# The first layer's attention modulation: sums of products on VectorE, or columns of matmuls on TensorE

## The chip, the cores and the metric

The kernel runs on one core of one Trainium2 chip. The metric is the device time of one execution in microseconds (us), as the median of several runs. TensorE is called PE here, VectorE DVE, ScalarE ACT, GpSimd POOL; SP is the sync engine, whose queue issues nearly all DMAs.

## The reference, cut to what matters

Two transformer layers, then a third of another kind. All is float32, with 256 tokens and width D = 1024. Each of the first two layers begins with

```
c_act = silu(c)
mod = c_act @ ada_w[l] + ada_b[l]                 # (1024) x (1024, 6144)
sh_a, sc_a, g_a, sh_f, sc_f, g_f = split(mod, 6)
h = rms_norm(x, attn_norm_g[l]) * (1 + sc_a) + sh_a
mix = hybrid_mixer(h, ...)                        # projections, two kinds of attention
```

Only the first 2048 columns of the first layer's `ada_w` (shift and scale of the attention norm) are touched by this change in how they are multiplied. The other 4096 columns of that layer follow during the first mixer.

## The kernel before

x is kept transposed: channels on the 128 partitions, eight tiles of 256 tokens (`xT`, `hT`). All weights come from one DRAM array in slots of 128 x 2048 floats (1 MB) into a ring of 14 slots, in the order of use; `Loads.load` issues a slot's DMA from SP, first waiting until the place's last owner has been used, `Loads.ready` makes an engine wait for its landing, and `used` counts slots that are done with.

`stage_setup` (L350 to L400) loads c as a row spread over all partitions, the vector of small parameters `vec`, the constants `tab` (identity, ones), x, and eight "ada" slots. Here a slot holds 256 output channels: an output channel on each partition, its 1024 weights along the row, two such halves. ACT takes Silu of the row. DVE multiplies each half with the row and sums along it (L326, `dve_modulation`), which gives one column of `mod`; 16 products for eight slots, the first six slots ahead of the reciprocal of the norm, two behind it. Beside that, ACT squares x tile by tile, PE sums the squares over channels with a matrix of ones (`pe_sum`, L463), and ACT takes the root. PE then runs 32 fillers (`keep_warm`, L316: identity times identity into an unused bank, two instructions each, as for every float32 product). At the end DVE adds the bias (L341) and makes the amp, g (1 + scale) (L346). SP queues the first two slots of the mixer and the first four of twelve "late" ada slots behind the eight.

`stage_mixer` for layer 0 starts behind a barrier of all engines. DVE scales x by amp and norm (L499), ACT adds the shift (L505), and PE runs through `items`: two output tiles a slot from slots 0 to 3, latent sums after the fifth item, queries and keys from slots 4 and 5, values, and two tiles a slot from slots 6 to 9. ACT copies each result out of its bank. DVE, meanwhile, has angles (waiting for the positions `posi`), a forget gate, a norm of the latents, the rotation, and between them the twelve late slots with `modulation(...)`. SP's order there is: positions, row of c again, mixer slots 2 to 9, late slots 4 to 7 (each waits until DVE is done with the slot four before), and behind the forget rows the late slots 8 to 11 and the mixer's last four. Attention and the output product follow, then the dense layer, the second mixer, two mixtures of experts and the third layer.

Of the kernel before, what the change touches and what calls it, by code (L numbers as in the profile page):

```python
# [8 lines left out]
ALU = mybir.AluOpType  # L9
ACT = mybir.ActivationFunctionType  # L10
# [4 lines left out]
P = 128  # L15
D = 1024
DT = D // P
T = 256
TT = T // P
SLOT = 2048  # L20
# [10 lines left out]
def vector_columns():  # L31

    cols = []
    for l in range(2):
        cols += [(f"ada_b{l}", 48), (f"attn_g{l}", 8), (f"ffn_g{l}", 8), (f"q_g{l}", 2), (f"kv_g{l}", 1),
                 (f"mla_g{l}", 4), (f"fox_g{l}", 4), (f"forget_b{l}", 1)]
    cols += [("final_g", 8), ("norm1", 8), ("norm2", 8), ("mu_prev", 14), ("mu_next", 14), ("decay0", 8),
             ("gate0", 8), ("k_k", 4), ("k_a", 4), ("r_k", 4), ("gn_w", 4), ("gn_b", 4), ("qn_g", 1),
             ("kn_g", 1), ("b_merge", 16)]
    at, out = 0, {}  # L40
    for name, n in cols:
        out[name] = slice(at, at + n)
        at += n
    return out, at
# [267 lines left out]
def keep_warm(k, bank, n):  # L312

    ident = k.t("ident")
    for _ in range(n):
        k.nc.tensor.matmul(bank[:, 0:P], ident, ident, start=True, stop=True)  # L316


def dve_modulation(k, dve, loads, slots, l, c_row, product, link, first=0):


    for j in slots:
        w = loads.ready(dve, j)
# [12 lines left out]
ADA_FIRST, ADA_LATE = 8, 12  # L336


def dve_bias(k, l, span, link):
    bias = k.vec[:, VEC[f"ada_b{l}"].start + span.start:VEC[f"ada_b{l}"].start + span.stop]  # L340
    link(k.nc.vector.tensor_tensor(k.mod[:, l, span], k.mod[:, l, span], bias, ALU.add))  # L341
# [5 lines left out]
                                          ALU.add, ALU.mult))  # L347


def stage_setup(k, loads, nxt, side):  # L350

    nc = k.nc
    small = k.counter("small_arrived")
    act_step = k.counter("act_step")
    x_arrived = k.counter("x_arrived")
    c_row, product = (k.hT[:, i:i + 4, :].rearrange("p t n -> p (t n)") for i in (0, 4))
    norm = StreamNorm(k, k.bank[0])
    with nc.Block() as block:
        @block.sync
        def _(sp):  # L360
            sp.dma_start(c_row, k.dram["c_row"].partition_broadcast(P)).then_inc(*small.up(16))
            sp.dma_start(k.vec[:, :], k.dram["vec"][:, :]).then_inc(*small.up(16))
            for j in range(4):
                loads.load(sp, j)
            sp.dma_start(k.tab[:, :], k.dram["tab"][:, :]).then_inc(*x_arrived.up(16))
            sp.dma_start(k.xT[:, :, :], k.dram["xT"][:, :, :]).then_inc(*x_arrived.up(16))
            for j in range(4, loads.n):
                loads.load(sp, j)
            sp.dma_start(k.router["router1"], k.dram["router1"][:, :, :]).then_inc(*k.counter("router_arrived").up(16))
            nxt.load(sp, 0)  # L370
            nxt.load(sp, 1)
            side.head(sp)

        @block.scalar
        def _(act):
            act.wait_ge(*small.at(32))
            nc.scalar.activation(c_row, c_row, ACT.Silu).then_inc(*act_step.up())
            act.wait_ge(*x_arrived.at(32))
            for t in range(DT):
                norm.act_square(act, t, k.xT[:, t, :])  # L380
            act.wait_ge(*norm.square_used.at(DT))
            norm.act_root(act)

        @block.tensor
        def _(pe):
            pe.wait_ge(*x_arrived.at(32))
            for t in range(DT):
                norm.pe_sum(pe, t, norm.bank, t == 0, t == DT - 1)
            keep_warm(k, k.bank[7], 32)

        @block.vector
        def _(dve):
            link = linker(dve, k.counter("dve_step"))
            dve.wait_ge(*act_step.at(1))
            dve_modulation(k, dve, loads, range(6), 0, c_row, product, link)
            norm.dve_inverse(dve, link)
            dve_modulation(k, dve, loads, range(6, ADA_FIRST), 0, c_row, product, link)
            dve_bias(k, 0, slice(0, 2 * ADA_FIRST), link)
            dve_amp(k, 0, 0, link)
    k.close()  # L400

# [146 lines left out]
def stage_mixer(k, l, loads, nxt, norm, nxt_norm, side=None):  # L548
    nc = k.nc
    S = k.counter  # L550
    dve_step, act_step = S("dve_step"), S("act_step")
    tile_done, tile_out = S("tile_done"), S("tile_out")
    with ExitStack() as ctx:
# [32 lines left out]
        forget_step, forget_moved = S("forget_step"), S("forget_moved")  # L586
        with nc.Block() as block:
            @block.sync
            def _(sp):
                sp.dma_start(k.posi[:, :], k.dram["pos1"].partition_broadcast(P)).then_inc(*S("small_arrived").up(16))  # L590
                if side is not None:
                    sp.dma_start(ada_c, k.dram["c_row"].partition_broadcast(P)).then_inc(*S("ada_arrived").up(16))
                    for j in range(2, 10):
                        loads.load(sp, j)
                    for j in range(side.slots, 2 * side.slots):
                        side.load(sp, j)
                sp.wait_ge(*S("pool_step").at(2))
                sp.wait_ge(*forget_step.at(4))
                sp.dma_start(qf[64:65, :, :], scratch[0:8, 6, :]).then_inc(*forget_moved.up(16))
                sp.dma_start(kf[96:97, :, :], scratch[0:8, 7, :]).then_inc(*forget_moved.up(16))  # L600
                if side is not None:
                    for j in range(2 * side.slots, side.n):
                        side.load(sp, j)
                    for j in range(10, loads.n):
                        sp.wait_ge(*side.done(side.n - side.slots + j - 10))
                        loads.load(sp, j)
                loads.rest(sp)
                sp.wait_ge(*forget_moved.at(32))
# [103 lines left out]
            def _(dve):  # L712
                v = nc.vector
                link = linker(dve, dve_step)

                def modulation(*js):
                    if side is not None:
                        if js[0] == 0:
                            dve.wait_ge(*act_step.at(1))
                        dve_modulation(k, dve, side, js, l, ada_c, ada_product, link, ADA_FIRST)  # L720
# [1 line left out]
                if l:  # L722
                    norm.dve_inverse(dve, link)
                norm.dve_scale(k.hT, k.amp[:, l, 0, :], norm.scaled)
                dve.wait_ge(*S("small_arrived").at(16))
                dve_angles(k, link, cos, sin, scratch[:, 0, :], scratch[:, 1, :], k.t("freq1"))
                v.tensor_copy(scratch[:, 2, :], cos[:, :]).then_inc(*S("angle_ready").up())
                modulation(0, 1)
                dve.wait_ge(*tile_out.at(4))
                link(v.tensor_scalar(z, misc[0:8, :], k.v(f"forget_b{l}")[0:8, :], None, ALU.add))  # L730
                link(v.tensor_scalar(lo, z, 0.0, None, ALU.min))
# [7 lines left out]
                for t in range(2):  # L739
# [1 line left out]
                                           ALU.mult).then_inc(*lat_ready.up())  # L741
                v.scalar_tensor_tensor(ckv[:, 0, :], ckv[:, 0, :], k.v(f"kv_g{l}", 0), k.rstd[:, 1, :], ALU.mult,
                                       ALU.mult).then_inc(*lat_ready.up())
                modulation(2, 3)
                dve.wait_ge(*forget_step.at(2))
                link(v.tensor_tensor(lo, lo, e, ALU.subtract))
                v.tensor_tensor_scan(F, k.t("ones")[0:8, 0:1].broadcast_to([8, T]), lo, 0.0, ALU.mult,
                                     ALU.add).then_inc(*forget_step.up())
                dve.wait_ge(*forget_step.at(3))
                v.tensor_scalar(negF, F, -1.0, None, ALU.mult).then_inc(*forget_step.up())  # L750
                modulation(4, 5)
                modulation(6, 7, 8)
                dve.wait_ge(*S("trig_ready").at(1))
                for i in range(5):
                    if i < 4:
# [718 lines left out]
TILE = 32  # L1474
QUADS = P // TILE
# [1881 lines left out]
def program(nc, dram, out):  # L3357
    with ExitStack() as ctx:
# [27 lines left out]
        def after(name):  # L3386
            if name == "mix1":
                return wide
            at = names.index(name) + 1
            return loads[names[at]] if at < len(names) else Loads(k.weights, 0)  # L3390

        stage_setup(k, loads["ada"], after("ada"), late_ada)
        norms = {name: (TokenNorm if name == "moe2" else StreamNorm)(k, k.bank[b]) for name, b in (
            ("mix0", 0), ("dense", 5), ("mix1", 4), ("moe1", 5), ("hybrid", 0), ("moe2", 0))}
        stage_mixer(k, 0, loads["mix0"], after("mix0"), norms["mix0"], norms["dense"], late_ada)
# [230 lines left out]
```

## Time and profile before

| | us |
|---|---|
| median of 3 runs | 2361.96 |
| lowest, highest | 2361.61, 2366.49 |
| the profiled execution | 2362.96 |
| its span, first to last instruction | 2360.7 |
| PE busy | 2185.4 (93% of the span) |
| DVE busy | 665.5 (28%) |
| ACT busy | 317.1 (13%) |

Times in the profile are counted from the first instruction. The rows below name the engine, the line, the operation and the tiles (out<-in); in brackets stand the idle time ahead of a group and what ended it. PE's float32 products appear as two instructions each.

### The profile page before, as it was taken

The page shows a single profiled execution, that of the slowest core. Times are in us where ns is not written, and L with a number is a line of the kernel's source. Part 1 is how long each engine was busy: PE and PEld are TensorE (multiplying, and loading weights), DVE is VectorE, ACT ScalarE, POOL GpSimd, SP SyncE. Part 2 cuts the span into 40 slices and gives each one's busy share as a digit, 9 for nine tenths or more (in the row PEclk, how much of TensorE's full clock was granted, in tenths as well). Part 3 has the DMA queues.
Part 4 walks back from the last instruction along what each step waited for, and adds up shares of the span by engine and source line. Part 5 has one row for each costly group of instructions (what it writes and reads, how often), then busy time and mean ns, then how long its engine had stood idle before and what let it go on. Part 6 is the DMA issues. An engine that isn't in the chain of part 4 may idle for free. (4 is left out here: it accounts for less than half of the span.)

```text
span 2360.7 us, 46236 instructions
## 1 busy us (share of the span) xinstructions
PE 2185.4 (93%) x21328; PEld 1336.0 (57%) x21328; DVE 665.5 (28%) x1237; ACT 317.1 (13%) x711; POOL 30.9 (1%) x30
## 2 busy tenths in 40 slices
PE   6999999999999999999999999999999997767776
PEld 5788888887734344443535353678889862212221
DVE  6863222344501101011011012237554331111110
ACT  2431000144200000000000000143232110000000
POOL 1000000010000000000000000100000000000000
PEclk9999999999999999999999999999999998777777
DMA  9668555701699999999999999634400679999998
GB/s 399 255 252 336 210 228 214 304 37 55 252 398 414 406 400 416 403 419 400 420 400 419 394 420 418 252 134 143 151 25 4 264 323 421 421 421 422 421 422 361
DMA packets 111595, 734.83 MB, mean 311 GB/s; under 512 B 12832, under 2 KB 16192, under 8 KB 36768
## 3 DMA queue, kind: packets, MB, share of 16 engines
q1 hardware_dynamic: 109456, 724.82, 75.8%
q8 instruction: 171, 2.80, 0.5%
q0 software_dynamic: 1152, 4.19, 0.4%
q10 hardware_dynamic: 784, 2.75, 0.3%
q14 instruction: 32, 0.26, 0.0%
HBM read 721.20 MB, written 10.09 MB: 310 GB/s over the span
## 5 line engine op out<-in xcount | busy, mean ns | idle before, releaser
L1550 PE MATMUL bank<-ring,moe_xg 128*32 128x512 f32 (+1 forms) x6144 | 580.8, 540 | 0.7 <-DVE moe_xg L1706 0.7
L1550 PEld LDWEIGHTS bank<-ring,moe_xg 128*32 128x32 f32 x6144 | 199.1, 110 | 377.1 <-issue 375.1
L1561 PE MATMUL bank<-ring,moe_turned 128*32 128x256 f32 x5376 | 291.5, 379 | 0.0
L1561 PEld LDWEIGHTS bank<-ring,moe_turned 128*32 128x32 f32 x5376 | 174.7, 110 | 117.1 <-issue 3.1
L1104 PE MATMUL bank<-h_chan,ring 128*128 128x256 f32 x896 | 195.6, 379 | 1.4 <-ACT h_chan L505 1.4
L1104 PEld LDWEIGHTS bank<-h_chan,ring 128*128 128x128 f32 x896 | 170.2, 190 | 24.7 <-issue 1.6
L2062 PE MATMUL bank<-ring,late 128*32 128x512 f32 x696 | 118.2, 779 | 56.1 <-DMA ring<-stream 56.0
L1745 DVE TENSOR_TENSOR moe_hidden<-moe_silu,bank 128x512 f32<-128x512 f32 (+1 forms) x48 | 26.9, 616 | 482.2 <-PE bank L1550 482.2
L2513 PE MATMUL bank<-h_chan,ring 128*128 128x256 f32 x624 | 137.2, 380 | 0.0
L2513 PEld LDWEIGHTS bank<-h_chan,ring 128*128 128x128 f32 x624 | 118.0, 190 | 18.9 <-issue 3.3
L2062 PEld LDWEIGHTS bank<-ring,late 128*32 128x32 f32 x696 | 17.5, 121 | 150.2 <-DMA ring<-stream 129.7
L1088 PE MATMUL bank<-dense_hidden,ring 128*128 128x256 f32 x448 | 98.8, 379 | 0.0
L1699 DVE COPY moe_y<-bank 32x256 f32<-32x256 f32 x48 | 20.0, 416 | 257.1 <-PE bank L1561 256.6
L1088 PEld LDWEIGHTS bank<-dense_hidden,ring 128*128 128x128 f32 x448 | 85.1, 190 | 11.6
L632 PE MATMUL bank<-h_chan,ring 128*128 128x256 f32 x384 | 84.0, 379 | 1.0 <-ACT h_chan L505 1.0
L2085 PE MATMUL bank<-ring,moe_turned 128*32 128x512 f32 x392 | 59.2, 708 | 26.5 <-DMA ring<-stream 25.5
L1607 ACT ACTIVATE moe_silu<-bank 128x512 f32<-128x512 f32 (+1 forms) x48 | 22.7, 545 | 434.5 <-PE bank L1550 434.5
L632 PEld LDWEIGHTS bank<-h_chan,ring 128*128 128x128 f32 x384 | 72.8, 190 | 11.8 <-issue 2.1
L2128 DVE TENSOR_TENSOR moe_hidden<-late,bank 128x512 f32<-128x512 f32 x8 | 5.5, 687 | 239.4 <-PE bank L2062 239.4
L326 DVE CUSTOM_DVE_ANT_0 ada_product<-ada_slots,ada_c 128x1024 f32<-128x1024 f32 x56 | 68.5, 1223 | 1.5
L1121 DVE TENSOR_TENSOR dense_hidden<-dense_silu,bank 128x512 f32<-128x512 f32 x14 | 9.6, 688 | 201.3 <-PE bank L1104 201.3
L1690 ACT ACTIVATE moe_y<-bank 32x256 f32<-32x256 f32 x48 | 18.1, 376 | 354.2 <-PE bank L1561 353.7
(461 smaller groups left out, 2064.4 us busy)
## 6 DMA issues: line engine op xcount, KB each, us to landing
ring<-stream SPq DMA_DIRECT2D x257, 1024.0 KB, 22.5
ring<-wide SPq DMA_DIRECT2D x240, 1024.0 KB, 15.9
ring<-wide SPq DMA_DIRECT2D x128, 768.0 KB, 15.8
late<-stream SPq DMA_DIRECT2D x47, 1024.0 KB, 27.0
ada_slots<-stream SPq DMA_DIRECT2D x28, 1024.0 KB, 7.1
h_chan<-stream SPq DMA_DIRECT2D x9, 1024.0 KB, 26.7
rows<-zeros SPq DMA_DIRECT2D x8, 512.0 KB
moe_x_rows<-rows SPq DMA_DIRECT2D x28, 96.0 KB, 9.0
```

The costliest lines, as they stand in the source:

```text
L326: mul = k.nc.vector.tensor_tensor_reduce(product, w[:, i * D:(i + 1) * D], c_row, 1.0, 0.0, ALU.mult, ALU.add, accum_out=k.mod[:, l, at:at ...
L632: mm = nc.tensor.matmul(b[:, 0:T], w[:, t, i * P:(i + 1) * P], k.hT[:, t, :], start=(t == 0), stop=(t == DT - 1))
L1088: mm = nc.tensor.matmul(k.bank[t // 2][:, (t % 2) * T:(t % 2) * T + T], w[:, f, t * P:(t + 1) * P], hidden[:, c % 2, f, :], start=(c == 0 ...
L1104: mm = nc.tensor.matmul(b[:, f * T:(f + 1) * T], w[:, t, f * P:(f + 1) * P], k.hT[:, t, :], start=(t == 0), stop=(t == DT - 1))
L1550: mm = self.k.nc.tensor.matmul(banks[r][i * TILE:(i + 1) * TILE, 0:width], self.m.xg[:, r, t * TILE:(t + 1) * TILE], w[:, i, :], start=(t ...
L1561: mm = self.k.nc.tensor.matmul(self.sum_bank[r][q * TILE:(q + 1) * TILE, :], self.m.turned[:, r, n * TILE:(n + 1) * TILE], w[:, f2, q * T: ...
L1607: k.nc.scalar.activation(m.silu[:, r, 0:self.span[c]], self.gate_bank[r][:, 0:self.span[c]], ACT.Silu)\
L1699: last = self.k.nc.vector.tensor_copy(self.m.y[r * TILE:(r + 1) * TILE, q * T:(q + 1) * T], self.sum_bank[r][q * TILE:(q + 1) * TILE, :])
L1745: v.tensor_tensor(m.hidden[:, r, 0:self.span[c]], m.silu[:, r, 0:self.span[c]], self.up_bank[r][:, 0:self.span[c]], ALU.mult).then_inc(*se ...
L2062: mm = k.nc.tensor.matmul((self.gate_bank if j < self.per_proj else self.up_bank)[own, :], m.xg[:, t, own], w[:, i, e, :], start=(t == 0), ...
L2085: mm = k.nc.tensor.matmul(k.bank[half][own, :], m.turned[:, f, own], w[:, i, e, :], start=(f == 0), stop=(f == 3))
L2513: mm = nc.tensor.matmul(b[:, 0:T], lhsT, rhs, start=(t == 0), stop=(t == DT - 1))
```

## The change

The eight ada slots of the first layer now hold rows by input channel: slot j has input channels 128j to 128j+127 on the partitions and all 2048 output channels along the row. c comes as eight columns inside `vec`, not as a row; ACT takes Silu of them, each spread over 32 columns (`c_blocks`, 128 x 8 x 32). PE multiplies for each slot four times, 128x32 by 512 columns, into four groups of 32 partitions of one bank, summed over the eight slots. One filler stands ahead of the first slot and eight ahead of each of the others. DVE copies the bank to SBUF, PE turns the rows to columns with four products against four columns of the identity, and DVE adds the bias. The reciprocal of the norm stands ahead of all that on DVE.

SP's order: `vec`, `tab`, x, the eight slots, positions, router, two mixer slots. The late slots leave the setup: in the mixer's block the row of c comes first, then late slots 0 and 1, then mixer slots 2 to 7 and late slots 2 to 7 in turn, then mixer slots 8 and 9. DVE takes late slot 2 ahead of the forget gate; 3 and 4, 5 and 6, 7 and 8 follow at the places after.

```diff
-def stage_setup(k, loads, nxt, side):
+def stage_setup(k, loads, nxt):
...
         def _(sp):
-            sp.dma_start(c_row, k.dram["c_row"].partition_broadcast(P)).then_inc(*small.up(16))
             sp.dma_start(k.vec[:, :], k.dram["vec"][:, :]).then_inc(*small.up(16))
-            for j in range(4):
-                loads.load(sp, j)
             sp.dma_start(k.tab[:, :], k.dram["tab"][:, :]).then_inc(*x_arrived.up(16))
             sp.dma_start(k.xT[:, :, :], k.dram["xT"][:, :, :]).then_inc(*x_arrived.up(16))
-            for j in range(4, loads.n):
+            for j in range(loads.n):
                 loads.load(sp, j)
+            sp.dma_start(k.posi[:, :], k.dram["pos1"].partition_broadcast(P)).then_inc(*posi_arrived.up(16))
...
             nxt.load(sp, 0)
             nxt.load(sp, 1)
-            side.head(sp)
...
-            act.wait_ge(*small.at(32))
-            nc.scalar.activation(c_row, c_row, ACT.Silu).then_inc(*act_step.up())
+            act.wait_ge(*small.at(16))
+            nc.scalar.activation(c_blocks, spread_last(k.v("c"), TILE), ACT.Silu).then_inc(*act_step.up())
...
                 norm.pe_sum(pe, t, norm.bank, t == 0, t == DT - 1)
-            keep_warm(k, k.bank[7], 32)
+            pe.wait_ge(*act_step.at(1))
+            for j in range(loads.n):
+                keep_warm(k, k.bank[7], 8 if j else 1)
+                w = loads.ready(pe, j)
+                for q in range(QUADS):
+                    mm = nc.tensor.matmul(row_bank[q * TILE:(q + 1) * TILE, :], c_blocks[:, j, :],
+                                          w[:, q * 512:(q + 1) * 512], start=(j == 0), stop=(j == DT - 1))
+                mm.then_inc(*((k.used, 1)))
+            pe.wait_ge(*rows_out.at(1))
+            for i in range(QUADS):
+                mm = nc.tensor.matmul(column_bank[:, i * QUADS:(i + 1) * QUADS], rows[:, i * P:(i + 1) * P],
+                                      k.t("ident")[:, 0:P:TILE], start=True, stop=True)
+            mm.then_inc(*turned.up())
...
-            dve.wait_ge(*act_step.at(1))
-            dve_modulation(k, dve, loads, range(6), 0, c_row, product, link)
             norm.dve_inverse(dve, link)
-            dve_modulation(k, dve, loads, range(6, ADA_FIRST), 0, c_row, product, link)
-            dve_bias(k, 0, slice(0, 2 * ADA_FIRST), link)
+            dve.wait_ge(*posi_arrived.at(16))
+            dve.wait_ge(*loads.done(loads.n - 1))
+            v.tensor_copy(rows, row_bank[:, :]).then_inc(*rows_out.up())
+            dve.wait_ge(*turned.at(1))
...
+            link(v.tensor_tensor(own, columns, bias, ALU.add))
             dve_amp(k, 0, 0, link)
...
-                if side is not None:
+                if side is None:
+                    sp.dma_start(k.posi[:, :], k.dram["pos1"].partition_broadcast(P))\
+                        .then_inc(*S("small_arrived").up(16))
+                else:
                     sp.dma_start(ada_c, k.dram["c_row"].partition_broadcast(P)).then_inc(*S("ada_arrived").up(16))
-                    for j in range(2, 10):
+                    side.load(sp, 0)
+                    side.load(sp, 1)
+                    for j in range(2, 8):
                         loads.load(sp, j)
-                    for j in range(side.slots, 2 * side.slots):
                         side.load(sp, j)
+                    for j in range(8, 10):
+                        loads.load(sp, j)
...
                 modulation(0, 1)
+                modulation(2)
...
-                modulation(2, 3)
+                modulation(3)
+                modulation(4)
...
-                modulation(4, 5)
-                modulation(6, 7, 8)
+                modulation(5, 6)
+                modulation(7, 8)
```

## Rows read from the trace of the kernel before

**Rows 1.** The page's head.
```profile
span 2360.7 us, 46236 instructions
```

**Rows 2.** Timeline, 0 to 75 us: start, duration, engine, line, operation, out<-in, count.
```profile
0.73 0.39 SPq L361 DMA_DIRECT2D h_chan<-c_row  x1
...
3.64 1.28 SPq L365 DMA_DIRECT2D tab_sb<-tab  x1
...
8.52 1.22 DVE L326 CUSTOM_DVE_ANT_0 h_chan<-ring,h_chan 128x1024 f32<-128x1024 f32 x1 [8.52 <-DMA ring<-stream]
...
19.47 1.03 ACT L458 ACTIVATE rstd<-x_chan 128x256 f32<-128x256 f32 x3 [12.63 <-DMA x_chan<-xT]
...
20.03 6.32 PE L463 MATMUL bank<-rstd,tab_sb 128*128 128x256 f32 x16 [20.03 <-ACT rstd L458]
...
22.06 1.23 DVE L326 CUSTOM_DVE_ANT_0 h_chan<-ring,h_chan 128x1024 f32<-128x1024 f32 x1 [3.44 <-DMA ring<-stream]
...
26.19 7.31 PE L316 MATMUL bank<-tab_sb 128*128 128x128 f32 x64
...
34.20 0.17 DVE L346 SCALAR_TENSOR_TENSOR amp<-mod,vec_sb 128x8 f32<-128x8 f32 x1
...
36.09 17.51 PE L632 MATMUL bank<-h_chan,ring 128*128 128x256 f32 x80
...
45.70 0.29 DVE L843 CAST score<-posi 128x256 f32<-128x256 int32 x1 [7.53 <-DMA posi<-pos]
```

**Rows 3.** Windows: engines' busy time, PEclk (granted), DMA share, GB/s.
```profile
0.00:6.00 6.00, 0.00 (x0) 0.00 (x0) 0.00 (x0) 1.50 (x2) 0.19 (x4) 1.00 0.62 202
6.00:20.00 14.00, 0.00 (x0) 0.00 (x1) 9.86 (x16) 1.37 (x3) 0.00 (x0) 1.00 1.01 426
20.00:34.00 14.00, 13.46 (x80) 12.12 (x80) 11.63 (x18) 4.34 (x9) 0.00 (x0) 1.00 1.01 418
```

**Rows 4.** Timeline at the end of the first mixer block.
```profile
92.06 13.98 PE L635 MATMUL bank<-ring,h_chan 128*128 128x256 f32 x64
...
103.29 0.17 DVE L346 SCALAR_TENSOR_TENSOR amp<-mod,vec_sb 128x8 f32<-128x8 f32 x1
106.07 0.38 ACT L697 ACTIVATE vf<-bank 128x256 f32<-128x256 f32 x1 [3.07 <-PE bank L635]
```

**Rows 5.** Line L463: ns min/median/max, first and last start.
```profile
L463 PE MATMUL bank<-rstd,tab_sb x16: 379/634/767, 20.0 to 26.0; 128*128 128x256 f32 x16
```

**Rows 6.** PE's timeline in the last stage, 1910 to 2000 us.
```profile
1918.12 7.07 PE L2062 MATMUL bank<-ring,late 128*32 128x512 f32 x64
1925.01 1.90 PE L2062 MATMUL bank<-late 128*32 128x512 f32 x16
...
1931.02 1.04 PE L2062 MATMUL bank<-ring,late 128*32 128x512 f32 x8
1931.99 0.44 PE L2031 MATMUL bank<-tab_sb,moe_gated 128*128 128x128 f32 x2
...
1934.49 1.95 PE L2046 MATMUL bank<-moe_pick,late 128*128 128x128 f32 x16
1936.37 2.78 PE L2085 MATMUL bank<-ring,moe_turned 128*32 128x512 f32 x24
```

**Rows 7.** Timeline of the last stage, 1990 to 2010 us: column products copied out.
```profile
1992.61 1.06 PE L2085 MATMUL bank<-ring,moe_turned 128*32 128x512 f32 x8 [0.80 <-DMA ring<-stream]
...
1993.74 0.69 DVE L2139 COPY moe_y<-bank 128x512 f32<-128x512 f32 x1 [9.21 <-PE bank L2085]
```

**Rows 8.** Timeline ahead of the last stage: small products, and DVE reading a bank.
```profile
1904.13 1.05 PE L518 MATMUL bank<-tab_sb,rstd 128*128 128x1 f32 x8
...
1907.54 0.22 DVE L1360 SCALAR_TENSOR_TENSOR moe_gl<-bank,moe_inverse,mod 128x4 f32<-128x4 f32 x1 [0.40 <-PE bank L1326]
```

**Rows 9.** DMA issues, 0 to 80 us: KB each, us to landing.
```profile
h_chan<-c_row SPq DMA_DIRECT2D x1, 512.0 KB, 3.7
```

More of the change, by code:

```diff
@@ L37, in vector_columns @@
     cols += [("final_g", 8), ("norm1", 8), ("norm2", 8), ("mu_prev", 14), ("mu_next", 14), ("decay0", 8),
-             ("gate0", 8), ("k_k", 4), ("k_a", 4), ("r_k", 4), ("gn_w", 4), ("gn_b", 4), ("qn_g", 1),
+             ("gate0", 8), ("c", 8), ("k_k", 4), ("k_a", 4), ("r_k", 4), ("gn_w", 4), ("gn_b", 4), ("qn_g", 1),
              ("kn_g", 1), ("b_merge", 16)]
@@ L347, in dve_amp @@
                                           ALU.add, ALU.mult))
-def stage_setup(k, loads, nxt, side):
[L352 to L356, printed above, removed]
+def stage_setup(k, loads, nxt):
+    nc, S = k.nc, k.counter
+    small, x_arrived, posi_arrived = S("small_arrived"), S("x_arrived"), S("forget_moved")
+    act_step, rows_done, rows_out, turned = S("act_step"), S("tile_done"), S("tile_out"), S("rot_done")
+    c_blocks = k.hT[:, 0, :].rearrange("p (t n) -> p t n", t=DT)
+    rows = k.hT[:, 4:6, :].rearrange("p t n -> p (t n)")
+    row_bank, column_bank = k.bank[6], k.bank[5]
     norm = StreamNorm(k, k.bank[0])
@@ L360, in _ @@
         def _(sp):
-            sp.dma_start(c_row, k.dram["c_row"].partition_broadcast(P)).then_inc(*small.up(16))
             sp.dma_start(k.vec[:, :], k.dram["vec"][:, :]).then_inc(*small.up(16))
-            for j in range(4):
-                loads.load(sp, j)
             sp.dma_start(k.tab[:, :], k.dram["tab"][:, :]).then_inc(*x_arrived.up(16))
             sp.dma_start(k.xT[:, :, :], k.dram["xT"][:, :, :]).then_inc(*x_arrived.up(16))
-            for j in range(4, loads.n):
+            for j in range(loads.n):
                 loads.load(sp, j)
-            sp.dma_start(k.router["router1"], k.dram["router1"][:, :, :]).then_inc(*k.counter("router_arrived").up(16))
+            sp.dma_start(k.posi[:, :], k.dram["pos1"].partition_broadcast(P)).then_inc(*posi_arrived.up(16))
+            sp.dma_start(k.router["router1"], k.dram["router1"][:, :, :]).then_inc(*S("router_arrived").up(16))
             nxt.load(sp, 0)
             nxt.load(sp, 1)
-            side.head(sp)
         @block.scalar
         def _(act):
-            act.wait_ge(*small.at(32))
-            nc.scalar.activation(c_row, c_row, ACT.Silu).then_inc(*act_step.up())
+            act.wait_ge(*small.at(16))
+            nc.scalar.activation(c_blocks, spread_last(k.v("c"), TILE), ACT.Silu).then_inc(*act_step.up())
             act.wait_ge(*x_arrived.at(32))
@@ L388, in _ @@
                 norm.pe_sum(pe, t, norm.bank, t == 0, t == DT - 1)
-            keep_warm(k, k.bank[7], 32)
+            pe.wait_ge(*act_step.at(1))
[11 more added lines that the diff above has]
+            mm.then_inc(*turned.up())
         @block.vector
         def _(dve):
-            link = linker(dve, k.counter("dve_step"))
-            dve.wait_ge(*act_step.at(1))
-            dve_modulation(k, dve, loads, range(6), 0, c_row, product, link)
+            v = nc.vector
+            link = linker(dve, S("dve_step"))
             norm.dve_inverse(dve, link)
-            dve_modulation(k, dve, loads, range(6, ADA_FIRST), 0, c_row, product, link)
-            dve_bias(k, 0, slice(0, 2 * ADA_FIRST), link)
+            dve.wait_ge(*posi_arrived.at(16))
+            dve.wait_ge(*loads.done(loads.n - 1))
+            v.tensor_copy(rows, row_bank[:, :]).then_inc(*rows_out.up())
+            dve.wait_ge(*turned.at(1))
+            own = k.mod[:, 0, 0:2 * ADA_FIRST].rearrange("p (g i) -> p i g", g=QUADS)
+            bias = k.v("ada_b0")[:, 0:2 * ADA_FIRST].rearrange("p (g i) -> p i g", g=QUADS)
+            columns = column_bank[:, 0:2 * ADA_FIRST].rearrange("p (i g) -> p i g", g=QUADS)
+            link(v.tensor_tensor(own, columns, bias, ALU.add))
             dve_amp(k, 0, 0, link)
@@ L589, in _ @@
             def _(sp):
-                sp.dma_start(k.posi[:, :], k.dram["pos1"].partition_broadcast(P)).then_inc(*S("small_arrived").up(16))
-                if side is not None:
+                if side is None:
+                    sp.dma_start(k.posi[:, :], k.dram["pos1"].partition_broadcast(P))\
+                        .then_inc(*S("small_arrived").up(16))
+                else:
                     sp.dma_start(ada_c, k.dram["c_row"].partition_broadcast(P)).then_inc(*S("ada_arrived").up(16))
-                    for j in range(2, 10):
+                    side.load(sp, 0)
+                    side.load(sp, 1)
+                    for j in range(2, 8):
                         loads.load(sp, j)
-                    for j in range(side.slots, 2 * side.slots):
                         side.load(sp, j)
+                    for j in range(8, 10):
+                        loads.load(sp, j)
                 sp.wait_ge(*S("pool_step").at(2))
@@ L724, in _ @@
                 norm.dve_scale(k.hT, k.amp[:, l, 0, :], norm.scaled)
-                dve.wait_ge(*S("small_arrived").at(16))
+                if side is None:
+                    dve.wait_ge(*S("small_arrived").at(16))
                 dve_angles(k, link, cos, sin, scratch[:, 0, :], scratch[:, 1, :], k.t("freq1"))
@@ L3390, in after @@
             return loads[names[at]] if at < len(names) else Loads(k.weights, 0)
-        stage_setup(k, loads["ada"], after("ada"), late_ada)
+        stage_setup(k, loads["ada"], after("ada"))
         norms = {name: (TokenNorm if name == "moe2" else StreamNorm)(k, k.bank[b]) for name, b in (
@@ L3544 @@
                       ("gate0", "a_gate0_2"), ("k_k", "k_k_2"), ("k_a", "k_a_2"), ("r_k", "r_k_2"),
-                      ("gn_w", "gn_w_2"), ("gn_b", "gn_b_2"), ("b_merge", "b_merge_2")):
+                      ("gn_w", "gn_w_2"), ("c", "c"), ("gn_b", "gn_b_2"), ("b_merge", "b_merge_2")):
         put(name, x[key])
@@ L3555 @@
     for l in range(2):
-        add(x["ada_w"][l].T.reshape(24, 2, P, D).transpose(0, 2, 1, 3).reshape(24, P, SLOT))
+        rows = 0
+        if l == 0:
+            add(x["ada_w"][0][:, 0:SLOT].reshape(DT, P, SLOT))
+            rows = SLOT
+        add(x["ada_w"][l][:, rows:].T.reshape(-1, 2, P, D).transpose(0, 2, 1, 3).reshape(-1, P, SLOT))
     def mixer(l):
```

## Prediction

> **What bounds the kernel now.** I read the page's head first [rows 1], then the first 45 us in order of time [rows 2], what the DMA engines moved there [rows 3], and the first mixer block's end [rows 4]. The reader is to see that after 36 us TensorE (PE) is the engine that everything waits for: the mixer's first products start at 36.09, its last ones (64 instructions of L635) run from 92.06 to 106.04, and ScalarE's last copy of them at 106.07 ends the block, with VectorE (DVE) done at 103.46 [rows 2, 4]. In those 70 us PE waits for nobody for more than 0.5 us at a time, and no slot is late. So the change is worth what it does to one moment: the end of the setup's amp at 34.20 + 0.17 = 34.37, which starts the scaling, the shift and, 1.7 us later, PE [rows 2]. Before that moment DVE is the bound: it waits for the fifth slot until 22.06 and then multiplies without a gap. All that follows hangs on PE's start, so I take a shift of that moment one to one to the end.
>
> **The transfers.** In the first 6 us 202 GB/s x 6 = 1.21 MB move, then about 0.42 MB per us [rows 3], so a slot of 1.05 MB every 2.49 us. Up to the first slot 1.71 MB were asked for (row of c, vec, slot), which the rates give at 7.2; DVE began on it at 8.52. Up to the fifth slot it is 7.42 MB, at 20.8; DVE began at 22.06 [rows 2]. Both lag by 1.3 us, and I use that as the landing delay. In the new order vec, tab and xT are 1.64 MB, so xT is there at 6 + 0.43/0.42 + 1.3 = 8.4; as the first microseconds could be slower with a table in front of them, 8.5. It was 19.47. The last of eight slots: 10.03 MB, 6 + 8.82/0.42 + 1.3 = 28.3.
>
> **PE before the slots.** The eight sums of squares took from 19.47 to the first filler at 26.19, 6.72 us [rows 2]. They ran mostly at the lower clock: the granted clock reads 1.00, but the L463 instructions last 634 ns in the median and 379 at the least [rows 5], and ScalarE's squares behind them are 0.85 us apart; that is the 1.2 GHz level, and PE had stood idle 20 us before. The same idle lies ahead of them after the change (8.5 us), so 6.72 again: PE reaches the slots at 15.2, with two of them landed.
>
> **PE at the slots.** Per slot there are now eight fillers (16 instructions of 128x128 by 128 columns) and four products of 128x32 by 512 columns in four column groups (8 instructions). Before has no such mixture in the setup, but its last stage has both halves with the switch between them [rows 6]: from the last set of eight L2062 to the next full-width instruction 1931.99 - 1931.02 = 0.97 us, and from 16 full-width instructions of L2046 to the next column set 1936.37 - 1934.49 = 1.88. Together 2.85 us a slot. That is more than the 2.49 us of its transfer, so PE never catches up with the loads. The first slot has one filler: 0.22 + 0.1 + 0.97 = 1.3. The slots end at 15.2 + 1.3 + 7 x 2.85 = 36.45, and the last set of products starts 0.97 ahead of it, at 35.5.
>
> Sets that follow each other show what the switch is: eight of them start 1925.01 - 1918.12 = 6.89 us apart, 0.86 each [rows 6], so 0.11 of the 0.97 us is the switch. With the same on the way back, 16 switches are 1.8 us in all. The Trainium skill has a rule for this that speaks against the change: on the page TensorEngine Tiling (Array Packing), section Key Properties, it says that going to another tiling mode, unlike going to another tile, drains the engine. The trace agrees, with 0.11 us for one. Without such a drain the sum would be 1.8 us less, by that rule it is as above.
>
> **The tail.** Nearest is the last stage, where a set of column products is copied out of PSUM: set at 1992.61, copy of 128x512 at 1993.74 for 0.69 [rows 7]. So copy at 35.5 + 1.13 = 36.6 to 37.3. The four turning products (8 instructions with full weights and 4 columns) are nearest to L518, eight of 128x1 in 1.05 us [rows 8]; 0.05 to start, 0.1 until DVE sees them: 38.5. Bias from PSUM: 0.22, as L1360 [rows 8]; 0.03; amp 0.17 [rows 2]. The amp ends at 39.0 in place of 34.37: **4.6 us later**. Bounds of the unknown pieces: the sums at the upper clock throughout would take 3.5 us instead of 6.7 (their products at half the price; the squares at 0.42 each keep up), which leaves 1.4; a clock that rises 3 us later than it did costs about 1.5 more, 6.1; xT half a microsecond either way.
>
> **What is removed.** DVE loses 16 products of 1.22 us and their reads, the broadcast row of c (0.5 MB, 1.25 us of transfer) and its Silu of 1.06 us. These were the bound from 22.06 to 34.37; PE's 21 us in a row take that place, so they give back nothing more than is in the sum. The bias and amp stay.
>
> **The mixer's part** I cost at nothing, and this is the cover. SP no longer queues four late slots in the setup; the last thing there is the second mixer slot, 12.3 MB in, at 33.7. The engines then stand idle until the block starts. The row of c, issued at 39.5, lands as it did from an idle queue in 3.7 us [rows 9], 43.2; late slots 0 and 1 and mixer slot 2 follow, 50.7. PE starts at 39.0 + 1.7 = 40.7 and wants slot 2 after four items of 3.5 us, 54.7: 4.0 us to spare. From then on two slots come per 5.0 us and PE takes 6.9 us for one of the mixer's (17.51 us for five items [rows 2]), so the margin grows. Late slots 4 to 7 now wait in SP's queue for DVE's use of late slots 0 to 3, and mixer slots 5 to 9 wait behind them. The last gate is that of late slot 7: it opens with the products on late slot 3, which follow the latent norm, some 28 us after PE's start (the norm's last row is 26 us after it now); mixer slot 8 behind it is wanted 56 us after. DVE's own chain: the positions came only at 45.70, after 7.5 us of waiting, and are now there at once, so the angles and late slots 0 and 1 move ahead, and the 2.5 us of late slot 2 in front of the forget gate end before PE has delivered the latent sums. Late slot 8 is issued behind the forget rows as before and lands about 45 us after PE's start; the products on it end 47.5 us after, as now (83.6 - 36.1). So DVE keeps its 3 us ahead of PE at the end [rows 4]. If a late slot cost more than those, each microsecond would count.
>
> **Sum.** The profiled execution took 2362.96 us, 2.3 more than its span of 2360.7 [rows 1], and the median of the three runs is 1.0 below it. 2362.96 + 4.6 = 2367.6, less 1.0 is **2366.6**. A change under 0.2% (4.7 us) can't be told from none here; the forecast lies just within, so its two halves count for same and slower.
>
> **Rivals.**
> (a) *The loads set the pace*: the fillers fit into the gaps between landings. Then the last set starts at 28.3, the copy at 29.4 and the amp ends at 31.8, 2.6 us earlier: 2359.4, still same. For it speaks that the fillers stand ahead of each wait; against it 2.85 against 2.49 us and a start with two slots behind. It holds only if a slot costs PE under 1.7 us: (28.3 - 16.5)/7. Chance 0.10.
> (b) *The lower clock lasts*: PE's first burst now comes after 8.5 us, with ScalarE's pace between its sums. Should the clock rise 6 us later than the 5 us it took before, 6 us of the sums and first slots pass at half the rate, 3 us more, 7.6 in all: 2369.6, slower. It decides from 0.1 us beyond my sum on. Against it stands that the burst and the idle time ahead of it are of the same kind as before. With it a mixer slot 2 late by over 4 us, which would need the row of c to land 4 us later than in 3.7. Chance 0.15.
> (c) *Faster by over 0.2%*: the mixer would have to give back 9 us; DVE's end is 3 us clear of PE's, so there is nothing to win. Chance 0.03.
> (d) *Nothing arrives*: a later stage paced by its loads swallows the delay. The middle stages are full of PE work, and the last one starts when its slots come free; 2362. Chance 0.04.
>
> **Chances.** The forecast with 2363.5 to 2368 has 0.68, of which 0.40 lie within 0.2% and 0.28 above. Same: 0.40 + 0.10 + 0.04 = 0.54; slower: 0.28 + 0.15 = 0.43; faster 0.03. The range that leaves out 2 in 10: the lower end between rival (a) and the forecast, 2361.0, the upper with rival (b) nearly whole, 2369.5.
>
> **What would show it.** xT's squares start near 8.5; PE is busy without a wait from 15 to 36, with pairs of 1.88 and 0.97; slots have landed by 29 and wait for PE; the amp ends at 39; the mixer's first products start at 40.7 and last 70 us. Wrong if a slot costs PE less than 2.5 us, if the first sums are over before 13, if PE waits in the mixer for slot 2, or if the end of the block doesn't move with its start.

## Result, and the profile after

The changed kernel is slower: 2370.34 us in the median of eight runs against 2364.25 of eight runs of the kernel before, ratio 1.0029 (95% interval 1.0020 to 1.0038), so 6.9 us (4.7 to 9.0). In a second comparison it was 1.0034 (1.0022 to 1.0046). One of the first eight runs of the changed kernel, at 4490 us, lies so far off that the ratio leaves it out.

The timeline of the kernel after, 0 to 48 us, answers to [rows 2]; its last row is taken from the view of 41 to 62 us:

```profile
9.00 1.03 ACT L473 ACTIVATE rstd<-x_chan 128x256 f32<-128x256 f32 x3 [5.68 <-DMA x_chan<-xT]
9.56 6.15 PE L478 MATMUL bank<-rstd,tab_sb 128*128 128x256 f32 x16 [9.56 <-ACT rstd L473]
15.54 0.38 PE L316 MATMUL bank<-tab_sb 128*128 128x128 f32 x2
15.86 1.07 PE L392 MATMUL bank<-ring,h_chan 128*32 128x512 f32 x8
16.85 2.05 PE L316 MATMUL bank<-tab_sb 128*128 128x128 f32 x16
18.84 1.06 PE L392 MATMUL bank<-ring,h_chan 128*32 128x512 f32 x8
19.83 2.05 PE L316 MATMUL bank<-tab_sb 128*128 128x128 f32 x16
...
36.70 1.06 PE L392 MATMUL bank<-ring,h_chan 128*32 128x512 f32 x8
37.94 0.69 DVE L408 COPY h_chan<-bank 128x512 f32<-128x512 f32 x1 [19.75 <-PE bank L392]
38.69 1.05 PE L397 MATMUL bank<-tab_sb,h_chan 128*128 128x4 f32 x8 [0.92 <-DVE h_chan L408]
39.78 0.18 DVE L413 TENSOR_TENSOR mod<-bank,vec_sb 128x16 f32<-128x16 f32 x1 [1.15 <-PE bank L397]
40.00 0.17 DVE L346 SCALAR_TENSOR_TENSOR amp<-mod,vec_sb 128x8 f32<-128x8 f32 x1
40.70 1.43 PE L316 MATMUL bank<-tab_sb 128*128 128x128 f32 x10 [0.96 <-PEq L359]
...
41.91 19.14 PE L652 MATMUL bank<-h_chan,ring 128*128 128x256 f32 x80
```

x is there at 9.00 instead of 19.47, and PE begins with the slots at 15.54. Then fillers and products follow each other without a bracket, which means without idle time: from set to set 18.84 - 15.86 = 2.98 us, and 36.70 - 15.86 is seven times that. DVE, which had been the bound, sits for 19.75 us until the last set is done. The amp ends at 40.17 in place of 34.37, 5.8 us later.

The second thing to see is the last row. The mixer's first 80 instructions took 17.51 us before [rows 2] and take 19.14 now. The windows over PE at their start (columns: stretch, length, busy and count, PEclk, DMA share, GB/s) say why:

```profile
41.90:45.20 3.30, 3.30 (x10) 0.50 0.89 292
45.20:48.50 3.30, 3.30 (x17) 0.99 1.02 425
```

PE is busy in both, but the granted clock in the first is 0.50, the 1.2 GHz level, and 10 instructions pass instead of 17. Ahead of it PE had done little from 37.76 to 40.70: 0.92 us of waiting for the copy, eight instructions of 4 columns, 0.96 us of waiting for the new block. The ten fillers at the start of the block still passed in 1.43 us, and the clock fell at their end. The end of the first mixer block, answering to [rows 4]:

```profile
99.52 13.98 PE L655 MATMUL bank<-ring,h_chan 128*128 128x256 f32 x64
...
110.62 0.17 DVE L346 SCALAR_TENSOR_TENSOR amp<-mod,vec_sb 128x8 f32<-128x8 f32 x1
113.53 0.38 ACT L717 ACTIVATE vf<-bank 128x256 f32<-128x256 f32 x1 [3.07 <-PE bank L655]
114.22 1.97 PE L908 MATMUL bank<-km,qm 96*128 96x256 f32 x8 [0.73 <-PEq L602]
```

The attention's first products before:

```profile
106.76 3.69 PE L885 MATMUL bank<-km,qm 96*128 96x256 f32 x16 [0.73 <-PEq L587]
```

The last copy at 113.53 stood at 106.07: 7.46 us later, which is 5.8 + 1.65. DVE's last row there ends 2.7 us ahead of it; before it was 2.6. The attention's first product here, at 114.22, stood at 106.76; it is the mark by which the experiments are compared. Like every mark it is read from one profiled execution of each run, while the times are medians of several.

### The profile page after: what moved, and what is told of

It reads as the page before. It is cut to its first block and busy times, and to the rows that moved or that the text cites. A ratio compares the mean times of both kernels' runs of the same rounds, so it can differ in the third digit from the quotient of the medians.

```text
span 2370.4 us, 46440 instructions
## 1 busy us (share of the span) xinstructions
PE 2202.0 (93%) x21450; PEld 1343.0 (57%) x21450; DVE 649.9 (27%) x1206; ACT 317.0 (13%) x711; POOL 30.9 (1%) x30
```

## The experiments

Theory A: PE sets the pace of the new setup, because eight fillers, four products and two changes of shape take more than the 2.49 us in which a slot lands; in its second part, the pauses of PE around the turning (the four products that turn rows to columns) let the clock fall. Theory B: the loads moved out of the setup cost the time. Theory C was added when a result did not fit. The marks of each run, in us; "amp" is its end, "80" the mixer's first 80 instructions:

| run | amp | 80 | attention | ratio to before (95%) |
|---|---|---|---|---|
| before | 34.37 | 17.51 | 106.8 | |
| after | 40.17 | 19.14 | 114.2 | 1.0029 (1.0020 to 1.0038) |
| e11_after_again | 39.40 | 18.36 | 113.4 | 1.0034 (1.0022 to 1.0046) |
| e2_fillers0 | 31.88 | 18.32 | 105.9 | one run, 2362.93 us |
| e8_nofill_timed | 34.27 | 18.12 | 108.3 | 1.0008 (0.9999 to 1.0017) |
| e1_fillers4 | 32.61 | 18.17 | 106.6 | 1.0012 (1.0003 to 1.0021) |
| e10_fillers16 | 51.02 | 17.50 | 123.4 | 1.0092 (1.0077 to 1.0107) |
| e6_same_shape | 36.26 | 17.77 | 110.0 | one run, 2367.03 us |
| e3_warm_tail | 38.41 | 17.50 | 110.9 | 1.0026 (1.0017 to 1.0035) |
| e5_both | 33.44 | 17.50 | 105.9 | 1.0006 (0.9997 to 1.0015) |
| e12_two_same_shape | 33.97 | 17.50 | 106.5 | 1.0002 (0.9993 to 1.0010) |
| e4_order_alone | 34.34 | 17.50 | 106.7 | 1.0000 (0.9991 to 1.0009) |
| e9_delay | 42.16 | 17.50 | 114.5 | 1.0042 (1.0029 to 1.0056) |
| e7_vec_pad | 34.74 | 17.50 | 107.1 | 1.0004 (0.9995 to 1.0013) |

**Four fillers a slot.**

```diff
-                keep_warm(k, k.bank[7], 8 if j else 1)
+                keep_warm(k, k.bank[7], 4 if j else 1)
```

> The changed kernel with four fillers ahead of each slot's products instead of eight. Theory A (the setup is paced by TensorE: fillers, products and the changes of shape take 2.98 us a slot): a slot takes 2.98 - 0.89 = 2.09 us, less than the 2.49 us of its transfer, so the loads set the pace; the last set of products starts near 29 instead of 36.70 and the amp ends 3.3 us after that, near 32.5 instead of 40.00 + 0.17. Time 7.7 us below the changed kernel if TensorE's clock in the mixer behaves as it did there, ratio to the kernel before 0.9995 (0.9985 to 1.0005). Theory B (the loads taken out of the setup, and the transfer engines idle between the blocks, cost the time): the setup is shorter, but the mixer waits for slots and gives it back; ratio stays above 1.002.

The timeline of this run, last two sets and what follows:

```profile
27.07 1.06 PE L392 MATMUL bank<-ring,h_chan 128*32 128x512 f32 x8
28.06 1.16 PE L316 MATMUL bank<-tab_sb 128*128 128x128 f32 x8
29.15 1.06 PE L392 MATMUL bank<-ring,h_chan 128*32 128x512 f32 x8
...
33.14 2.31 PE L316 MATMUL bank<-tab_sb 128*128 128x128 f32 x10 [0.96 <-PEq L359]
35.25 18.17 PE L652 MATMUL bank<-h_chan,ring 128*128 128x256 f32 x80
```

A slot takes 2.08 us, the last set starts at 29.15 and the amp ends at 32.61: theory A's numbers, and theory B falls, for the mixer does not wait. One step of the expectation was not so: the loads don't set the pace here. From the first set at 14.56 to the last no row has a wait in front of it, so PE, which began behind its loads, still sets the pace and only just catches up. The gain of 1.8 us over the kernel before is gone by the attention, since the block's fillers and 80 instructions take 1.6 us more than before at the lower clock. But the time is 1.0012 of before, though attention starts 0.2 us earlier than there; theory A had 0.9995. That is theory C's ground, below.

**No fillers**, in one execution (e2) and in a timed run (e8).

```diff
-                keep_warm(k, k.bank[7], 8 if j else 1)
```

> The changed kernel without any filler between the slots. Theory A: loads set the pace as with four; the products of a set run at 1.2 GHz (1.73 us instead of 0.86), which still fits into 2.49 us; the last set starts near 29, the amp ends near 33.5; the mixer's first products run at the lower clock for some microseconds, costing 1.5 to 3 us there. Theory B: nothing is gained over the changed kernel at the end of the first mixer block (its first attention product at 114.2).

> No fillers between the slots, timed. Its one execution had attention at 105.9 and 2362.93 in all. Theory A: 0.9 us under the kernel before plus nothing, ratio 0.9996. Theory C: 2 us over it, ratio 1.0009.

The timeline of the first of them:

```profile
17.63 1.07 PE L391 MATMUL bank<-ring,h_chan 128*32 128x512 f32 x8 [1.00 <-DMA ring<-stream]
20.12 1.06 PE L391 MATMUL bank<-ring,h_chan 128*32 128x512 f32 x8 [1.42 <-DMA ring<-stream]
22.59 1.94 PE L391 MATMUL bank<-ring,h_chan 128*32 128x512 f32 x8 [1.41 <-DMA ring<-stream]
...
27.55 1.93 PE L391 MATMUL bank<-ring,h_chan 128*32 128x512 f32 x8 [0.54 <-DMA ring<-stream]
```

From the fourth on each set waits for its slot, 2.47 to 2.49 us apart, as worked out from the transfers. Three sets ran at the lower clock (1.93 in place of 1.06 us; the granted clock from 22.5 to 28 us is 0.50) and still fit. The amp ends at 31.88, and at 34.27 in the second execution, in which x and the slots landed 1.6 us later and the turning took 1.87 in place of 1.05 us. The time, 1.0008, can't be told from that of the kernel before; it is what theory C expected, but with the attention 1.6 us late in this execution it doesn't decide for it.

**Sixteen fillers a slot.**

```diff
-                keep_warm(k, k.bank[7], 8 if j else 1)
+                keep_warm(k, k.bank[7], 16 if j else 1)
```

> The changed kernel with sixteen fillers a slot instead of eight. Theory A: each slot takes 1.79 us more, 4.77, seven of them 12.5 us; the last set starts near 49.2 and the amp ends near 52.7; the time is 12.5 us above the changed kernel, ratio to the kernel before 1.008 (1.007 to 1.0095). Theory B: fillers lie in waits for slots, and the amp moves by clearly less than 12 us.

```profile
15.20 3.84 PE L316 MATMUL bank<-tab_sb 128*128 128x128 f32 x32
18.97 1.07 PE L392 MATMUL bank<-ring,h_chan 128*32 128x512 f32 x8
19.97 3.84 PE L316 MATMUL bank<-tab_sb 128*128 128x128 f32 x32
...
51.55 1.35 PE L316 MATMUL bank<-tab_sb 128*128 128x128 f32 x10 [0.96 <-PEq L359]
```

A slot takes 19.97 - 15.20 = 4.77 us, as expected. The amp ends at 51.02, not 52.7, because the first sums started at 8.00 here and at 9.56 in the execution it was worked out from. With 4, 8 and 16 fillers the slot is 2.08, 2.98 and 4.77: fillers are paid one to one while PE is behind the loads. The last row is for later: these are the mixer's ten fillers, at the upper clock (1.35 us as before).

**Fillers in the products' shape.**

```diff
-                keep_warm(k, k.bank[7], 8 if j else 1)
+                for _ in range(8 if j else 1):
+                    nc.tensor.matmul(k.bank[7][0:TILE, 0:P], c_blocks[:, 0, :], k.t("ident"), start=True, stop=True)
```

> The changed kernel with its eight fillers a slot in the shape of the products (weights 128x32 into one column group, 128 columns), so that TensorE doesn't change shape between fillers and products. Theory A with the change of shape as a cost of 0.1 us or more each way: a slot takes 16 x 0.107 + 0.86 = 2.6 us (2.55 to 2.75) instead of 2.98, the amp ends 2.6 us earlier in the same time after x has landed. If the change of shape costs nothing and the 2.98 are the instructions themselves: 2.9 us or more.

```profile
16.98 0.63 PE L393 MATMUL bank<-ring,h_chan 128*32 128x512 f32 x3
...
18.05 1.80 PE L390 MATMUL bank<-tab_sb,h_chan 128*32 128x128 f32 x15
19.58 0.63 PE L393 MATMUL bank<-ring,h_chan 128*32 128x512 f32 x3
```

The same 16 + 8 instructions take 2.60 us a slot in one shape and 2.98 in two. So 0.38 us of each slot, 2.7 us of seven, belong to the changes of shape and what goes with them: more than the 0.22 that I had read from the last stage.

**The clock around the turning.**

```diff
+            keep_warm(k, k.bank[7], 4)
             pe.wait_ge(*rows_out.at(1))
...
             mm.then_inc(*turned.up())
+            keep_warm(k, k.bank[7], 3)
```

> The changed kernel with four more fillers between the last slot's products and the turning, and three behind the turning. Theory A, its second part (the pauses of TensorE around the turning let the clock fall to 1.2 GHz in the mixer's first 3 us): the amp ends where it did, 40.2 (40.0 to 40.4); the mixer's first 80 instructions take 17.5 us as before instead of 19.14, and attention starts 1.6 us earlier than at 114.2; ratio to the kernel before 1.0022. If the lower clock there has another cause (the shape of the work ahead of it, or chance), the 80 instructions keep 19.1 us.

> The changed kernel once more, beside the others on one chip. Theory A: amp between 38.4 and 40.2 (with x landing between 8 and 9), the mixer's 80 instructions over 18 us again because of the pauses around the turning; ratio 1.0026 (1.002 to 1.0035). If the slow 80 instructions were chance: 17.5 us.

The last rows of the run with these fillers, then the windows over its first products:

```profile
37.84 0.91 PE L316 MATMUL bank<-tab_sb 128*128 128x128 f32 x6
38.24 0.17 DVE L346 SCALAR_TENSOR_TENSOR amp<-mod,vec_sb 128x8 f32<-128x8 f32 x1
39.05 1.35 PE L316 MATMUL bank<-tab_sb 128*128 128x128 f32 x10 [0.30 <-PEq L359]
40.24 17.50 PE L654 MATMUL bank<-h_chan,ring 128*128 128x256 f32 x80
```

```profile
40.20:43.50 3.30, 3.30 (x17) 1.00 0.93 298
```

The amp ended at 38.41, not near 40.2, because the sums began at 8.47 and took 5.3 us, against 9.56 and 6.0 in the execution the expectation was worked out from. So the amp says nothing on the fillers, and the stretch behind it is what counts. From the end of the amp to the attention it is 114.2 - 40.2 = 74.0 us in the changed kernel, 74.0 in its repetition and with four fillers, 74.0 and 74.1 in the runs without any, and 73.7 in the one with the other shape. It is 72.5 in every run with fillers around the turning (e3, e5, e12) and 72.4 in the kernels that turn nothing (before, e4, e9, e7). The second part of theory A holds: where the clock falls, it costs 1.3 to 1.7 us against 72.4. One run stands apart: with sixteen fillers a slot and the same pauses it is 72.4 too, so a pause makes the fall possible and not sure. In the time the 1.6 us can't be seen: 1.0026 against 1.0029 and 1.0034, with intervals of 0.0009 to 0.0012 either way.

**The order alone**, in the kernel before: late slots out of the setup, positions in, mixer and late slots in turn, and the new places on DVE.

```diff
+            sp.dma_start(k.posi[:, :], ...)
...
-            side.head(sp)
...
+                    side.load(sp, 0)
+                    side.load(sp, 1)
+                    for j in range(2, 8):
                         loads.load(sp, j)
                         side.load(sp, j)
```

> The kernel before with the new order alone: late slots out of the setup, positions in it, mixer and late slots in turn, and the new places of the late products on VectorE; the modulation of the first layer stays on VectorE. Theory A: costs nothing, the amp ends at 34.4 and attention starts at 106.7 within 0.4 us; ratio 1.000. Theory B: attention starts 2 us or more later, ratio 1.001 or more.

```profile
34.86 1.35 PE L316 MATMUL bank<-tab_sb 128*128 128x128 f32 x10 [2.35 <-PEq L358]
36.05 17.50 PE L638 MATMUL bank<-h_chan,ring 128*128 128x256 f32 x80
```

Attention at 106.7 and ratio 1.0000: the order costs nothing, as the prediction had it. The first row shows in passing that 2.35 us without any work, behind 64 dense instructions of fillers, left the clock up.

**What lies behind the mixer (theory C).** Two kernels on the base of the one before: eight unused columns in `vec`, and a delay.

```diff
-             ("gate0", 8), ("k_k", 4), ...
+             ("gate0", 8), ("spare", 8), ("k_k", 4), ...
```

> The kernel before with eight unused columns in the vector of parameters, where the change puts c, so that all that lies behind it in SBUF moves by 32 bytes a partition. Theory C with the layout as its cause: attention starts at 106.7 as before, but the end comes 2 to 4 us later, ratio 1.0013. Theory A, or C with another cause: ratio 1.000.

```diff
-            keep_warm(k, k.bank[7], 32)
+            keep_warm(k, k.bank[7], 64)
...
             dve_bias(k, 0, slice(0, 2 * ADA_FIRST), link)
+            for _ in range(6):
+                link(nc.vector.tensor_tensor(product, product, product, ALU.max))
```

> The kernel before with six more VectorE products of 1.23 us ahead of the amp (they change nothing that is read) and 32 more fillers on TensorE beside them, so that the amp ends 7.6 us later and TensorE is as busy ahead of the mixer as before. A delay there goes one to one to the end: 7.6 us later, ratio 1.0032 (1.0024 to 1.004). If the stages behind take part of a delay up, or add to it, it is under 5 or over 10 us.

The layout's 1.0004 (0.9995 to 1.0013) speaks against it as the cause but doesn't exclude it: theory C asked for 1.0013. A pure delay moves the amp and the attention by 7.8 us and the end by 9.9 us (6.9 to 13.2), so one to one is within its interval and not more than that is known. Of the 9.9 us some 1.4 lie outside the span from first to last instruction: device time less span is 3.6 us in this kernel, 2.2 to 2.3 in the one before, and 1.8 in all that have the products on PE.

One place where executions differ behind the mixer can be read from PE's timeline at the start of the first mixture of experts; first before, then e3, then e5:

```profile
640.25 22.23 PE L1550 MATMUL bank<-ring,moe_xg 128*32 128x512 f32 x192 [0.65 <-DVE moe_xg L1706]
```

```profile
644.81 23.54 PE L1575 MATMUL bank<-ring,moe_xg 128*32 128x512 f32 x192 [0.65 <-DVE moe_xg L1731]
```

```profile
639.98 23.33 PE L1575 MATMUL bank<-ring,moe_xg 128*32 128x512 f32 x192 [0.65 <-DVE moe_xg L1731]
```

In the second 3 us of this row the granted clock is 1.00 before and 0.57 in e3. It isn't the change that decides it: the same changed kernel has 22.15 us there in its first profiled execution and 23.57 in its repetition. From that row to the end of the span it is 1720.5 us in the profiled execution of the kernel before and 1730.4 in the run e5. Over the 14 profiled executions the same stretch goes from 1720 to 1730, and the one of before is at the low end.

That scatter belongs to single executions; a median of several is surer than that, so it doesn't settle theory C. If one sets each ratio against how far the attention moved, the end comes later than the attention alone would have it in seven of the eight comparisons with the products on PE, by 1.8 us in the mean of the eight, by 3.0 in e1 and by 5.1 in e10, and in e1, e5 and e10 the whole interval of the ratio lies above what the attention alone would give. In the three kernels with the products on DVE (e4, e7, e9) the mean is 0.9. As each attention is one execution, theory C stays open.

**Both mends.** Four fillers with the fillers around the turning, and two fillers of the products' shape with them.

```diff
-                keep_warm(k, k.bank[7], 8 if j else 1)
+                for _ in range(2):
+                    nc.tensor.matmul(k.bank[7][0:TILE, 0:P], c_blocks[:, 0, :], k.t("ident"), start=True, stop=True)
```

> Four fillers a slot and the fillers around the turning together. Theory A: amp near 32 as with four fillers, the mixer's 80 instructions take 17.5 us instead of 18.2, attention starts near 105.5, 1.2 us ahead of the kernel before: ratio 0.9995. Theory C (behind the first mixer block something adds 3 us to each kernel that has the products on TensorE, as it stood with four fillers, where attention started 0.2 us earlier than before and the end came 2.9 us later): ratio 1.0008.

> A version meant to beat both: two fillers a slot in the shape of the products, and the fillers around the turning. TensorE needs 1.3 us a slot, so that the loads set the pace; the last set starts near 29, the amp ends near 32.2, the mixer's 80 instructions take 17.5 us, attention starts near 104.6, 2.2 us ahead of the kernel before: ratio 0.9991 if that goes one to one to the end, 1.000 to 1.001 if what was seen behind the mixer with four fillers returns.

The end of the second one's setup:

```profile
25.07 1.06 PE L393 MATMUL bank<-ring,h_chan 128*32 128x512 f32 x8 [1.01 <-DMA ring<-stream]
...
29.10 1.94 PE L393 MATMUL bank<-ring,h_chan 128*32 128x512 f32 x8 [2.54 <-DMA ring<-stream]
30.96 1.79 PE L316 MATMUL bank<-tab_sb 128*128 128x128 f32 x8
```

Neither beats the kernel before: 1.0006 and 1.0002. Theory A had 0.9995 and 0.9991, theory C 1.0008 and 1.000 to 1.001, so both results are nearer to theory C. In the second, the last slot came 4.03 us behind the one ahead, not 2.49. Its set still started near 29, as expected, because x and the slots ahead had landed early. But the clock fell in that wait: set and fillers ran at the lower clock, and from the set's start to the end of the amp it took 4.87 us, against 3.46 with four fillers (e5). So 1.9 us of the 2.2 expected at the attention were gone: it starts 0.3 us before that of the kernel before, and in this run theory A itself would give 0.9999.

## Why the prediction was wrong

The direction and the place were right, the size was not: forecast 2366.6 within 2361.0 to 2369.5, measured 2370.34, above the range by 0.8 us. Slower by over 0.2% had a chance of 0.43, a change below that 0.54. Two steps failed in the mechanism, the mixer's part costed at nothing and the price of a slot at PE; besides, the time to which the change was added was too low.

- *PE sets the pace of the slots*: right. No bracket between 15.54 and 37.76, and a filler costs what it lasts in e1 and e10. Rival (a) asked for under 1.7 us a slot; it was 2.98.
- *A slot at PE, 2.85 us*: mis-sized. It measured 2.98, seven times 0.13 = 0.9 us. The term taken too low was the change of shape. From full-width instructions to a set I had taken 1.88 us from the last stage; here it is 1.99, and from the set to the next filler 0.99 in place of 0.97. By e6 the two changes of a slot and what goes with them are 0.38 us; the prediction, which had worked out one way and taken the other to be equal, had 0.22. The Trainium skill's rule (TensorEngine Tiling (Array Packing), Key Properties) is that changing the tiling mode drains the engine; e6 agrees, but no run shows that the 0.38 us are the drain itself.
- *x at 8.5*: 9.00 in the profiled execution; the first sums, at 9.56 in it, start between 8.0 and 9.8 in the others. With the length of the sums it moves the amp, from 38.4 to 40.2 in three runs with the same setup work: the sums of both repetitions (e3, e11) took 0.7 us less than in the first run, and those of e3 began 1.1 us earlier as well. The range had half a microsecond for x.
- *The sums, 6.72 us*: 6.54, counted from x. *The tail*, from last set to the amp's end, 3.5 us: 3.47.
- *"The mixer's part I cost at nothing"*: this step failed. I had followed slots, queues and DVE there, and all of that held (e4). I left out PE's own pauses around the turning, though the tail's terms put nearly 3 us of light work there. The clock at 1.2 GHz, in the mixer's first microseconds or the fillers ahead of them, cost 1.6 us here. Of the seven runs with these pauses six lost 1.3 to 1.7 us in this way and one (e10) nothing.
- *Rival (b), the lower clock*: the right kind at another place. I looked for it in the sums ahead of the slots, where it was much as before (from PE's first sum to what follows 5.98 us, 6.16 before).
- *One to one to the end*: not contradicted for the changed kernel. The attention moved by 7.5 us, and 6.6 in the repetition; the ratios are 6.9 (4.7 to 9.0) and 8.0 us (5.2 to 10.9).
- *The base*: the sum starts from 2361.96, the median of three runs; all eight give 2364.25, 2.3 us more. So of the 3.7 us between 2366.6 and 2370.34, 2.3 are the base and 1.4 the change. On the right base the forecast would have been 2368.9, and the measured time within a range moved along with it; the two errors of mechanism would not have shown in the number alone.

4.6 + 0.9 + 0.5 for x - 0.2 for sums and tail is 5.8 at the amp; with 1.6 for the clock it is 7.4 at the attention, 2.8 us more than forecast. In the medians 6.1 of it arrive; 0.5 us are given back outside the span (device time less span is 1.8 us, 2.3 in the kernel before), the rest is inside the intervals. What stays open: e1, with attention 0.2 us early, ended 2.8 us late (0.7 to 5.0), and the sources of the scatter behind the mixer were not taken apart further. Why the last slot landed late in e12 was not tried either.

## What to carry to other kernels

Fillers that keep a clock up are work like any other once the engine is behind its loads: add a filler's time to the work per load and compare it with the load's own time before choosing the count, and count how many loads have landed before the engine starts, for it has to catch up on those too. Where PE gets a new step whose result another engine has to copy and return, look at the pauses around it and at the granted clock of the stage behind, not only at the step. And read a price for two kinds of work in turn from rows in which they stand in just that turn; the nearest rows gave little over half of it.

## What was not expected of the hardware

- The granted clock fell to 0.50 behind a stretch of about 2.9 us in which PE was not without work (eight instructions of 4 columns, 1.05 us, between two pauses of 0.9 us) and ten dense fillers; behind the same stretch in e10 it stayed at 1.00. 2.35 us of idle time with dense fillers ahead of it (e4) did not bring it down either.
- In the run with two small fillers, PE could start on the last of eight equal slots only 4.03 us after the one ahead; the slots ahead that it waited for were 2.48 and 2.49 us apart. From 26 to 28 us that run's DMA moved 161 to 167 GB/s, with 419 ahead and 432 behind. But e2 and e8 have such a dip at that time too (181 to 194 and 153 to 158 GB/s), and there the last slot came 2.47 us after the one ahead.
- Two VectorE operations of 128x256, of which the first took 0.35 us before, took 1.86 us each in the mixer after, each while one of GpSimd's memsets ran; before, VectorE had been waiting for the positions at that time. They take 1.86 us in e4 and e9 too. It cost nothing here, for VectorE still ended 2.7 us ahead. The timeline after:

```profile
44.25 1.84 POOL L635 MEMSET qf<- 1x2048 f32 x1
44.38 1.86 DVE L867 TENSOR_SCALAR score<-score,tab_sb 128x256 f32<-128x256 f32 x1
```
